# Conditioned hybrid decoder layer on one core: another form for the first modulation products

## What is computed

```python
mod = (silu(c) @ w_ada + b_ada)[:, None, :]          # 9 rows of c: one prompt, eight samples
sh1, sc1, gt1, sh2, sc2, gt2 = split(mod, 6)
h = rmsnorm(x, g_mix) * (1 + sc1) + sh1              # needs sh1 and sc1: 2048 of the 6144 columns
z = h @ w_in                                         # every later product waits for h
```

## Time and profile before

| | us |
|---|---|
| median of 3 runs | 2066.27 |
| lowest and highest | 2062.45, 2068.49 |
| the profiled execution | 2060.58 |
| its span, first to last instruction | 2058.8 |
| busy: PE | 1993.9 (97%) |
| busy: DVE, ACT, POOL | 757.0, 460.8, 147.6 |
| mean granted TensorE clock | 0.975 |

### The profile page before, as it was taken

The page is one execution under the profiler, slowest core; times in us unless marked ns, Lnnn a source line. Parts: engine busy times, 40 slices in busy tenths (PEclk is TensorE's granted clock), DMA queues, the critical chain, the costliest instruction groups (busy, mean ns, idle before and its releaser), DMA issues.

```text
span 2058.8 us, 28749 instructions
## 1 busy us (share of the span) xinstructions
PE 1993.9 (97%) x11753; PEld 1922.5 (93%) x11753; DVE 757.0 (37%) x1332; ACT 460.8 (22%) x646; POOL 147.6 (7%) x251
## 2 busy tenths in 40 slices
PE   7999999999999999999999978999999999999997
PEld 7999998999999997777999967999999999999997
DVE  4322222222333342224634556423432442343246
ACT  3132222222433332222212112111111111111113
POOL 0001008300000012230000003000000000000000
PEclk7699999999999999999999989999999999999999
DMA  7545334452243436544632310111111111111112
GB/s 257 176 161 160 124 126 130 136 155 77 89 124 99 118 115 157 172 150 142 188 99 70 95 52 21 52 41 41 41 51 41 41 50 41 41 45 47 41 51 87
DMA packets 224146, 200.85 MB, mean 98 GB/s; under 512 B 13251, under 2 KB 202487, under 8 KB 224079
## 3 DMA queue, kind: packets, MB, share of 16 engines
q1 hardware_dynamic: 214958, 166.31, 27.1%
q10 hardware_dynamic: 7721, 29.25, 3.5%
q0 software_dynamic: 1408, 4.46, 0.7%
HBM read 150.19 MB, written 49.92 MB: 97 GB/s over the span
## 4 chain that ended last, share of the span: by engine, by line
PE 95%; DVE 3%; ACT 1%; issue 1%; DMA 1%; SPq 0%; DVEq 0%; ACTq 0%
PE dense L1729 80%; PE misc L1808 2%; PE misc L2017 2%; PE misc L2004 1%; PE misc L1943 1%; PE misc L1947 1%; PE misc L1916 1%; PE misc L1945 1%; PE misc L1841 1%; PE misc L1840 1%; PE misc L1926 1%; PE misc L2116 0%; DVE stage L1170 0%; DVE act_lo L1177 0%; PE dense L2116 0%
## 5 line engine op out<-in xcount | busy, mean ns | idle before, releaser
L1729 PE MATMUL dense<-act_hi,w_hi 128*128 128x384 f32 (+1 forms) x2808 | 647.8, 339 | 21.2 <-DVE act_lo L1177 18.6
L1729 PE MATMUL dense<-act_lo,w_hi 128*128 128x384 f32 (+1 forms) x2808 | 623.0, 330 | 0.0
L1729 PE MATMUL dense<-act_hi,w_lo 128*128 128x384 f32 (+1 forms) x2808 | 622.1, 329 | 0.0
L1729 PEld LDWEIGHTS dense<-act_hi,w_hi 128*128 128x128 f32 x2808 | 482.4, 189 | 45.1 <-issue 26.8
L1729 PEld LDWEIGHTS dense<-act_lo,w_hi 128*128 128x128 f32 x2808 | 483.5, 189 | 0.0
L1729 PEld LDWEIGHTS dense<-act_hi,w_lo 128*128 128x128 f32 x2808 | 483.0, 189 | 0.0
L1162 DVE TENSOR_TENSOR w_lo<-raw,w_hi 128x1024 fp32r<-128x1024 f32 x139 | 172.8, 1244 | 462.8 <-ACT w_hi L809 462.0
L809 ACT ACTIVATE w_hi<-raw 128x1024 fp32r<-128x1024 f32 x139 | 146.9, 1058 | 396.0 <-PE dense L1729 395.6
L1661 DVE SCALAR_TENSOR_TENSOR hmT<-dense,mod,hmT 128x768 f32<-128x768 f32 x80 | 81.4, 1017 | 69.2 <-PE dense L1729 68.6
L1729 PE MATMUL dense<-a_hi,w_lo 128*128 128x384 f32 (+1 forms) x480 | 106.3, 329 | 0.0
L1729 PE MATMUL dense<-a_lo,w_hi 128*128 128x384 f32 (+1 forms) x480 | 105.7, 328 | 0.0
(11 more groups left out here) (296 smaller groups left out, 1480.4 us busy)
## 6 DMA issues: line engine op xcount, KB each, us to landing
z_scratch<-stage ACTq DMA_DIRECT2D x52, 544.0 KB, 2.7
raw<-in_w_in_dram SPq DMA_DIRECT2D x53, 512.0 KB, 3.8
ada_w<-in_w_ada_dram SPq DMA_DIRECT2D x24, 1024.0 KB, 5.3
raw<-in_w_gate_up_dram SPq DMA_DIRECT2D x44, 512.0 KB, 3.7
stage<-z_scratch SPq DMA_DIRECT2D x24, 544.0 KB, 3.7
raw<-in_w_down_dram SPq DMA_DIRECT2D x22, 512.0 KB, 3.5
qkv<-z_scratch SPq DMA_DIRECT2D x8, 1024.0 KB, 6.8
cs<-in_state_mlstm_c_dram SPq DMA_DIRECT2D x32, 256.0 KB, 5.2
```

Of the source, the lines that this page charges most:

```text
L1729: ins = pe.matmul(tile(k, c), w[:, n % 2, off:off + P], x[:, xr, t0:t1], start=(first and p == 0), stop=(last and p == 2))
```

## The change

The ten early blocks are multiplied the other way round. The nine columns of `cT` are held and 256 columns of weights stream: 8 float32 products a block (16 records), and the result is nine rows of 256. Those of blocks 1 to 7 go to banks 3 to 5 of `dense`, those of 0, 8 and 9 to `misc`. ACT copies the nine rows to SBUF (`rows_of_mod`, semaphore `mrow_ready`) into two row buffers, and PE turns them with two transposes (`mod_turn`) into the place that `early_mod` reads. The turning of block e comes after the product of block e+1; that of block 0 after the last token tile, that of block 7 after the first set of `two_units`. The root's broadcast comes after block 1 instead of after block 2. A slot is free for the next load when ACT has copied the rows. Block 9 takes slot 1, and the first late block waits for the copy of block 6. The spill of `xT` goes behind blocks 8 and 9, two weight blocks and the first late block. The first two weight blocks are split in pair 0 instead of in pair 1. POOL also waits for the turning of block 9.

```diff
+ADA_SLOT = (0, 1, 2, 0, 1, 2, 0, 1, 2, 1)
+ADA_PSUM = (None, 3, 4, 3, 4, 3, 4, 5, None, None)
+R_PROD = {0: R_ADA, 8: R_ADA + 9, 9: R_ADA + 11}
+R_MOD = {e: R_ADA + 1 + e if e < 8 else R_ADA + 2 * e - 6 for e in range(10)}
+R_L1 = R_ADA + 13
...
 def late_ada_load(j, i=0, per=0):      # SP
...
-                    wait_full(sp, round_full, R_L1 - 1)
+                    sp.wait_ge(mrow_ready, 7)
...
 def ada_load(e):                       # SP
-                if e >= ADA_RING:
-                    wait_full(sp, round_full, R_ADA + e - ADA_RING)
...
+                if e >= 3:
+                    sp.wait_ge(mrow_ready, max(j for j in range(e) if ADA_SLOT[j] == ADA_SLOT[e]) + 1)
...
-            sp.wait_ge(xt_free, TT)
-            sp.dma_start(z[Z_X:Z_X + KT].rearrange("k p t -> p k t"), xT[:, :, :]).then_inc(x_spilled, 16)
             for e in range(ADA_FIRST, len(ADA_EARLY)):
                 ada_load(e)
             for j in range(2):
                 load(2 + j, w_cols(w_in[0], P * (1 + j)))
             late_ada_load(0)
+            sp.wait_ge(xt_free, TT)
+            sp.dma_start(z[Z_X:Z_X + KT].rearrange("k p t -> p k t"), xT[:, :, :]).then_inc(x_spilled, 16)
             late_ada_load(1)
...
+            def rows_of_mod(e):        # ACT
+                if e in R_PROD:
+                    wait_full(act, round_full, R_PROD[e])
+                else:
+                    act.wait_ge(eprod_full, e)
+                if e >= 2:
+                    wait_full(act, round_full, R_MOD[e - 2])
+                act.activation(mod_rows[e % 2], ada_bank(e), ACT.Copy).then_inc(mrow_ready, 1)
...
+            rows_of_mod(0)             # after the squares
...                                    # the two roots
+            rows_of_mod(1)
...                                    # the copies of the broadcast root
+            rows_of_mod(2)
+            pair_high(0)
+            split_hi(0)
+            split_hi(1)
+            for e in (3, 4, 5):
+                rows_of_mod(e)
+            pair_high(1)
+            for e in (6, 7):
+                rows_of_mod(e)
+            pair_high(2)
+            pair_high(3)
+            for e in (8, 9):
+                rows_of_mod(e)
...
-            early_mod(0)               # DVE, before the roots
...
-                if p:
-                    early_mod(2 * p)
+                early_mod(2 * p)
                 early_mod(2 * p + 1)
...
-                if p == 1:             # before the low parts of the pair
-                    split_lo(0)
-                    split_lo(1)
...
+                if p == 0:             # after them
+                    split_lo(0)
+                    split_lo(1)
...
+            def ada_rows_product(e):   # PE
+                j = ADA_SLOT[e]
+                pe.wait_ge(eada_in[j], 16 * (1 + sum(1 for i in range(e) if ADA_SLOT[i] == j)))
+                if e in R_PROD:
+                    take(R_PROD[e])
+                elif e == 1:
+                    pe.wait_ge(xt_free, TT - 1)
+                elif e > 2:
+                    pe.wait_ge(mrow_ready, e - 1)
+                w = ada_slots[j]
+                for kk in range(KT):
+                    ins = pe.matmul(ada_bank(e), cT[:, kk, :], w[:, kk, :], start=(kk == 0), stop=(kk == KT - 1))
...
+            def mod_turn(e):
+                r = R_MOD[e]
+                pe.wait_ge(mrow_ready, e + 1)
+                take(r)
...
-            early_ada(0)
+            ada_rows_product(0)
             for j in range(4, TT):
                 turn_x(j)
-            early_ada(1)
-            early_ada(2)
+            mod_turn(0)
+            ada_rows_product(1)
             pe.wait_ge(xt_free, TT)
             pe.wait_ge(diag_ready, 1)
             sum_partitions(T_SS, diag1)
-            for e in range(3, ADA_FIRST):
-                early_ada(e)
+            for e in range(2, ADA_FIRST):
+                ada_rows_product(e)
+                mod_turn(e - 1)
+            pe.wait_ge(mrow_ready, ADA_FIRST)
...
             def late_of_early(kk):
+                if kk == 0:
+                    mod_turn(ADA_FIRST - 1)
                 if kk in (2, 5):
-                    early_ada(ADA_FIRST + (kk == 5))
+                    ada_rows_product(8 + (kk == 5))
+                if kk in (3, 6):
+                    mod_turn(8 + (kk == 6))
```

More of the change, by code:

```diff
@@ L69 @@
 ADA_FIRST = KT
-X_RING, ADA_RING = 3, 3
-R_L1 = R_ADA + len(ADA_EARLY)
+ADA_SLOT = (0, 1, 2, 0, 1, 2, 0, 1, 2, 1)
+ADA_PSUM = (None, 3, 4, 3, 4, 3, 4, 5, None, None)
+X_RING = 3
+R_PROD = {0: R_ADA, 8: R_ADA + 9, 9: R_ADA + 11}
+R_MOD = {e: R_ADA + 1 + e if e < 8 else R_ADA + 2 * e - 6 for e in range(10)}
+R_L1 = R_ADA + 13
 L1_CUTS = ((0, 2), (2, 4), (4, 6), (6, 8), (8, 14))
@@ L168, in trunk @@
         ada_slots = (ada_w[:, 0, :, :], ada_w[:, 1, :, :], ada_w2[:, :, :])
+        mod_rows = [xtok[0:GRP, 2 + j, 0:256] for j in range(2)]
         diag1 = xtok[:, 0:2, :].rearrange("p j d -> p (j d)")[:, 0:T]
@@ L286, in trunk @@
         x_in = [sem(f"x_in{j}") for j in range(TT)]
-        eada_in = [sem(f"eada_in{j}") for j in range(ADA_RING)]
+        eada_in = [sem(f"eada_in{j}") for j in range(3)]
+        eprod_full, mrow_ready = sem("eprod_full"), sem("mrow_ready")
         xt_full, xt_free = sem("xt_full"), sem("xt_free")
@@ L358, in bank, with ada_bank @@
             return misc[0:rows, r % 2, 0:n]
+        def ada_bank(e):
+            if e in R_PROD:
+                return bank(R_PROD[e], 256, GRP)
+            return dense[0:GRP, ADA_PSUM[e], 0:256]
         def x_banks(j):
@@ L412, in ada_load @@
             def ada_load(e):
-                if e >= ADA_RING:
-                    wait_full(sp, round_full, R_ADA + e - ADA_RING)
-                sp.dma_start(ada_slots[e % ADA_RING], w_cols(w_ada[0], 256 * ADA_EARLY[e], 256)
-                             ).then_inc(eada_in[e % ADA_RING], 16)
+                if e >= 3:
+                    sp.wait_ge(mrow_ready, max(j for j in range(e) if ADA_SLOT[j] == ADA_SLOT[e]) + 1)
+                sp.dma_start(ada_slots[ADA_SLOT[e]], w_cols(w_ada[0], 256 * ADA_EARLY[e], 256)
+                             ).then_inc(eada_in[ADA_SLOT[e]], 16)
             def x_load(j):
@@ L681, in _ @@
             pool.wait_ge(h_ready, KT)
+            wait_full(pool, round_full, R_MOD[9])
             pool.wait_ge(x_spilled, 16)
@@ L841, in _, with pair_high @@
                                ).then_inc(xsq_ready, 1)
+            def rows_of_mod(e):
[6 more added lines that the diff above has]
+                act.activation(mod_rows[e % 2], ada_bank(e), ACT.Copy).then_inc(mrow_ready, 1)
+                if e in R_PROD:
+                    act.wait_ge(mrow_ready, e + 1)
+                    act.sem_inc(round_free[R_PROD[e] % 2], 1)
+            def pair_high(p):
+                act.wait_ge(hs32_ready, 3 * p + 3)
+                act.activation(act_hi[:, 2 * p:2 * p + 2, SEQ:T], stage[:, :, SEQ:T], ACT.Copy).then_inc(hhi_ready, 1)
+                for k in (2 * p, 2 * p + 1):
+                    act.wait_ge(h32_ready, k + 1)
+                    act.activation(act_hi[:, k, 0:SEQ], stage[:, k % 2, 0:SEQ], ACT.Identity, bias=mod[:, SH1 + k, 0:1]
+                                   ).then_inc(hhi_ready, 1)
+            rows_of_mod(0)
             act.wait_ge(consts_ready, 3)
@@ L852, in _ @@
             act.sem_inc(tile_free[T_SS % 2], 1)
[L853 to L859, removed]
-                if p == 1:
-                    split_hi(0)
-                    split_hi(1)
+            rows_of_mod(2)
[11 more added lines that the diff above has]
+                rows_of_mod(e)
             act.wait_ge(h_ready, KT)
@@ L1213, in early_mod @@
             def early_mod(e):
-                r, m = R_ADA + e, 2 * ADA_EARLY[e]
+                r, m = R_MOD[e], 2 * ADA_EARLY[e]
                 wait_full(dve, round_full, r)
@@ L1232, in _ @@
                 k0 = 2 * p
-                if p:
-                    early_mod(2 * p)
+                early_mod(2 * p)
                 early_mod(2 * p + 1)
                 for e in (2 * p, 2 * p + 1):
-                    wait_full(dve, round_free, R_ADA + e)
+                    wait_full(dve, round_free, R_MOD[e])
                 link(dve.scalar_tensor_tensor(out=amp1[:, k0:k0 + 2, :], in0=mod[:, SC1 + k0:SC1 + k0 + 2, :], scalar=1.0,
@@ L1798, in col_sums @@
                 give(ins, r)
-            def early_ada(e):
-                r = R_ADA + e
-                pe.wait_ge(eada_in[e % ADA_RING], 16 * (e // ADA_RING + 1))
+            def ada_rows_product(e):
+                j = ADA_SLOT[e]
+                pe.wait_ge(eada_in[j], 16 * (1 + sum(1 for i in range(e) if ADA_SLOT[i] == j)))
+                if e in R_PROD:
+                    take(R_PROD[e])
[6 more added lines that the diff above has]
+                    ins = pe.matmul(ada_bank(e), cT[:, kk, :], w[:, kk, :], start=(kk == 0), stop=(kk == KT - 1))
+                if e in R_PROD:
+                    give(ins, R_PROD[e])
```

(9 more changed lines are left out.)

## The result

The changed kernel takes 2039.98 us, the median of 4 runs (2039.46 to 2041.72), against 2065.58 us for 4 runs of the kernel before (2062.45 to 2068.49). The ratio is 0.9878, with a 95% interval of 0.9861 to 0.9895: 25.6 us faster, where 23.9 were forecast.

What follows compares the result with a forecast made beforehand. PE was taken as the bound, at half clock between 24 and 111 us because of the blocks' form. 19.1 us before `two_units` plus 4.8 in it give 23.9; 2066.3 - 23.9 = 2042, range 2034 to 2055.

Steps and rivals of the forecast that it cites:

- The product at 3.5 us and full clock: Early blocks: 16 records of 256 streamed columns take 3.5 us a block at full clock, against 6.86 today.
- The second rival: Early blocks: nine held columns do not lift the clock, a block stays 6.9 us, 2066, no change; 14%.
- That the stream breaks at every record: Third rival, early blocks: loads of held columns cannot slip under the stream; 8.3 us a block, 2077; 6%.
- The clock before the change: Kernel before: PE between 24 and 111 us is at half speed because of the blocks' form, not missing work.
- Start of `two_units` at 55.1: End of the head: PE reaches the first set of `two_units` at 55.1 instead of 74.2, 19.1 us earlier.
- `two_units` at 31.9: Stretch up to the first late block: 144 records, blocks 8 and 9, three turnings; 31.9 for 36.7, 4.8 less.
- The sum: Whole kernel: 19.1 + 4.8 = 23.9 us reach the end whole; 2066.3 - 23.9 = 2042; 70%.
- The spill's move at nothing: Spill behind block 9 and 2 MB more lands at 81.3, wanted at 83.7: nothing lost, 2.4 us to spare.
- The broadcast and the splits: Head: broadcast after block 1 takes 1.9 us instead of 3.84; high parts and two weight splits end at 41.7.
- pair 0's 5.3 us: Head: pair 0 starts at 34.2 instead of 39.47, 5.3 us earlier.
- The first rival: Around block 5: PE's waits of 1.2 and 1.1 us let the clock fall, 8.4 us back, 2050; 10%.

Runs made afterwards that it cites:

- form alone: Changed kernel with broadcast behind block 2, splits in pair 1 and spill before blocks 8 and 9, as in the kernel before; 2044.7 us, ratio 0.9906.
- order alone: Kernel before with broadcast after block 1, splits in pair 0, spill behind blocks 8, 9 and two weight blocks, products in the old form; 2061.5 us, ratio 0.9984.
- spill_before_8: Changed kernel with the spill of the tokens back in its old queue place, before blocks 8 and 9; 2045.9 us, ratio 0.9903.
- before_again: The kernel before, unchanged, run for a second trace; 2064.6 us, ratio 0.9998.
- own_turn: Changed kernel with each block's turning right behind its own product; 2043.6 us, ratio 0.9886.

## Why the prediction was right, step by step

- **The product at 3.5 us and full clock: right** (3.55 and 1.00). The row that carried it was the one with 64 held columns; nine held columns keep the clock up as well. The second rival falls with this, and with the two orders: form alone gives 20.9 us, order alone 4.3. That the stream breaks at every record falls with a pitch of 0.222 us.
- **The clock before the change: right where the sum uses it, too wide as it is put.** PE is not at half speed all the way from 24 to 111 us. The granted clock is 1.00 from 24 to 28 us and from 90 to 96 us, and 0.69 on the mean.
- **Start of `two_units` at 55.1: measured 56.34.** Of the 1.2 us, 1.0 is there at block 1 (25.20 for 24.2), where I took no wait for the copy of token tile 7: PE waited 1.3 us, and the tokens came later. From there each step is within 0.5 us: the broadcast 2.0 for 1.9, waits of 0.94 and 1.57 for 1.2 and 1.1, for the reasons named.
- **`two_units` at 31.9: measured 32.9.** Its 144 records take 25.2 us instead of 24.0: each change between kinds of records costs some 0.2 us, which I left out.
- **The sum.** Against the trace that it was made from, 23.9 us was too much: that trace gives 21.65 us at the first late block (1.2 us are missing at the start, 1.0 in `two_units`) and 20.5 at the end. The gain does not reach the end whole. Behind `two_units` the two traces of the kernel before take 1946 and 1948 us, the ten with the new form 1949 to 1951 and the one with the order alone 1949; no run shows why. The medians give 25.6 us, more than any pair of these two traces and the two of the changed kernel shows (18.3 to 23.5): both traces of before are executions below its median. The 5.7 us between the first of them and that median were carried as if they lay outside the change. The second trace, 3.0 us longer, is already 4.8 us later at the first late block, so a part at least of the 5.7 us lies in the stretch that the change shortens. That the number came out within 2 us is thus partly luck: two errors offset each other.
- **The spill's move at nothing: right, but the question was put too narrowly.** It is hidden where it went. What the prediction did not ask is what it would cost to leave it: 5.9 us by the medians, of which the trace shows 4.7 at block 8, since the faster head reaches block 8 before the transfers of the old order do.
- **The broadcast and the splits.** I credited pair 0's 5.3 us to the head as a whole; the broadcast's place is some 1 us of it at most, and the splits' place makes no difference that the medians show.
- **The first rival, a clock that falls in the waits: true, at other places.** Around block 5 the clock stayed at 1.00 (waits of 0.94 and 1.57 us). It fell near the start of block 1 in five of ten traces (1.5 to 1.7 us each), and in or just behind the waits of 2.8, 3.2 and 4.2 us in three variants. The Trainium skill (TensorE: Matmul & The Clock Gate, HAM oscillation) describes bursts of products that lose the clock in waits for transfers; `spill_before_8` agrees, with 5.01 us for a block that takes 3.55. In the kernel that the Trainium skill describes there, a burst of some 2 us is shorter than the wait for the transfer behind it. Around block 5 a product of 3.55 us is longer than either wait, so the prediction put a case under that rule which is not the one described.

## What to carry to other kernels

Ask of a product with one thin operand which side streams: at full clock both forms cost the same here (3.47 and 3.55 us), and the difference is what the clock does during and behind them. When a head gets faster, look at every transfer that it now overtakes, and put the large one behind those that are wanted first. In a queue that releases loads, the short copy that releases belongs ahead of the long work.

## What was not expected

The form that lets the clock fall seems to make the time uncertain too: the kernel before spreads over 8 us (2060.45 to 2068.37 in 13 runs), the changed one over 3.2 us in eight runs and the version with copy 3 first over 1.1 in four. This is shown in part only: `before_again` has its difference in the head, but `own_turn`, in the new form, spreads over 5.6 us in four runs. And an isolated wait costs more than itself: 3.2 us of waiting for a block cost 4.7 us, the wait and the block at the low clock.
